# A hybrid encoder layer with 32 experts: gathering tokens from the fp32 residual rows, and a shorter way from the residual to the choice of experts

## The reference

```
n = rms_norm(x, mix_norm_g);  z = n @ w_in               # 1024 x 2336
o = concat(GLA(z), GQA(z))                               # two groups of heads, 1024 wide
h = x + o @ w_out                                        # 1024 x 1024
m = rms_norm(h, ffn_norm_g)
logits = m @ w_router + b_router                         # 32 experts
top_val, top_idx = top_k(logits, 4); gates = softmax(top_val)
for each token and each of its 4 experts e:
    u = m @ w1[e] + b1[e]                                # 1024 x 2048
    a = min(u[:1024], 7); b = clip(u[1024:], -7, 7)
    y += gate * ((a * sigmoid(1.702 a) * (b + 1)) @ w2[e] + b2[e])   # 1024 x 1024
out = rms_norm(h + y, final_norm_g)
```

## Time and profile before

| | |
|---|---|
| median of 3 runs | 1094.7 us (1090.6 to 1095.1) |
| profiled execution, its own time | 1092.27 us |
| its span, first to last instruction | 1090.3 us |
| mean granted TensorE clock | 0.986 |
| TensorE busy, matmuls | 983.2 us, 90% |
| VectorE, ScalarE, GpSimd busy | 230.1, 117.4, 20.3 us |
| moved by DMA | 421.31 MB, mean 386 GB/s |

### The profile page before, as it was taken

How to read it: one execution, slowest core, us unless ns; L and a number is a source line. 1 busy time by engine, 2 the same in 40 slices (tenths; PEclk the granted TensorE clock), 3 DMA queues, 4 the chain that set the end, 5 groups by cost and what they waited for, 6 DMA issues and landing times.

```text
span 1090.3 us, 13890 instructions
## 1 busy us (share of the span) xinstructions
PE 983.2 (90%) x5869; PEld 425.6 (39%) x5869; DVE 230.1 (21%) x531; ACT 117.4 (11%) x226; POOL 20.3 (2%) x24
## 2 busy tenths in 40 slices
PE   6997878999999999988889888998988888898885
PEld 4644544344444444433333333333333333333332
DVE  1577344111111111111111001111111111110113
ACT  1053130000000000000000000000000000000002
POOL 0010020000000000000000000000000000000000
PEclk9998998999999999999999999999999999999998
DMA  9924746999999999999999999999999999999993
GB/s 319 287 110 209 308 154 253 429 421 417 394 426 426 429 427 429 429 427 429 429 429 428 429 428 429 428 429 429 429 429 428 429 428 429 428 429 429 429 429 161
DMA packets 33093, 421.31 MB, mean 386 GB/s; under 512 B 4880, under 2 KB 5136, under 8 KB 7376
## 3 DMA queue, kind: packets, MB, share of 16 engines
q1 hardware_dynamic: 33072, 421.02, 92.6%
HBM read 419.95 MB, written 1.05 MB: 386 GB/s over the span
## 4 chain that ended last, share of the span: by engine, by line
PE 49%; DMA 42%; DVE 5%; ACT 2%; issue 1%; POOL 0%; SPq 0%; POOLq 0%; DVEq 0%
DMA ring<-in_w_dram 41%; PE bank L1354 20%; PE bank L1388 12%; PE bank L1057 4%; PE bank L1325 3%; PE bank L1318 3%; PE bank L1265 1%; PE bank L1370 1%; ACT work L573 1%; PE bank L1253 1%; PE bank L1274 1%; DMA h<-in_x_dram 1%; ACT work L522 1%; PE bank L1198 0%; PE bank L1143 0%
## 5 line engine op out<-in xcount | busy, mean ns | idle before, releaser
L1354 PE MATMUL bank<-ring,work 128*64 128x512 f32 x2016 | 458.0, 598 | 51.2 <-DMA ring<-in_w_dram 50.0
L1354 PEld LDWEIGHTS bank<-ring,work 128*64 128x64 f32 x2016 | 166.6, 136 | 324.2 <-issue 210.7
L1388 PE MATMUL bank<-ring,work 128*64 128x512 f32 x1024 | 226.8, 595 | 15.5 <-ACT work L573 15.5
L975 DVE TENSOR_SCALAR work<-bank 128x512 f32<-128x512 f32 x32 | 22.1, 692 | 726.9 <-PE bank L1354 726.9
L1388 PEld LDWEIGHTS bank<-ring,work 128*64 128x64 f32 x1024 | 71.2, 137 | 150.5 <-issue 132.9
L570 ACT ACTIVATE work<-work 128x512 f32<-128x512 f32 x32 | 20.2, 632 | 539.1 <-DVE work L975 539.1
L1325 PE MATMUL bank<-work 64*128 64x512 f32 x256 | 63.6, 615 | 0.7 <-ACT work L581 0.7
L1318 PE MATMUL bank<-work,tok 128*128 128x64 bf16 x1056 | 50.8, 194 | 0.0
L1318 PE MATMUL bank<-work 128*128 128x64 bf16 x528 | 49.0, 195 | 1.2 <-DVE work L948 1.2
L1318 PEld LDWEIGHTS bank<-work,tok 128*128 128x128 bf16 x1056 | 47.4, 99 | 0.0
L1318 PEld LDWEIGHTS bank<-work 128*128 128x128 bf16 x528 | 33.7, 99 | 27.2 <-issue 27.2
(11 more groups left out here) (190 smaller groups left out, 487.8 us busy)
## 6 DMA issues: line engine op xcount, KB each, us to landing
ring<-in_w_dram SPq DMA_DIRECT2D x190, 2048.0 KB, 33.1
ring<-in_w_in_dram SPq DMA_DIRECT2D x8, 1168.0 KB, 18.7
work<-in_w_dram SPq DMA_DIRECT2D x2, 2048.0 KB, 12.0
ring<-in_w_out_dram SPq DMA_DIRECT2D x2, 1024.0 KB, 14.5
ring<-in_w_out_dram SPq DMA_DIRECT2D x1, 2048.0 KB, 21.1
h<-in_x_dram SPq DMA_DIRECT2D x2, 512.0 KB, 4.7
out_dram<-tok SPq DMA_DIRECT2D x4, 256.0 KB, 2.4
tok<-in_b_dram SPq DMA_DIRECT2D x3, 256.0 KB, 16.6
```

The costliest lines, as they stand in the source:

```text
L975: nc.vector.tensor_scalar(glu, bank[2][:, :], LIMIT, None, ALU.min).then_inc(S.glu_ready, 1)
L1354: last = mm(bank[(2, 5)[g]][j * CAP:(j + 1) * CAP, :], xg[:, k * CAP:(k + 1) * CAP], chunk[:, r, g * FF + j * FG:g * FF + (j + 1) * FG], s ...
L1388: last = mm(bank[6][j * CAP:(j + 1) * CAP, :], hidT[:, r, s * CAP:(s + 1) * CAP], chunk[:, r, j * 512:(j + 1) * 512], start=s == 0 and r == 0,
```

## The change

The rows are no longer normalised and split. The gather takes the fp32 residual rows `h` themselves as weights, and the one-hot matrix, now fp32, holds 1/rms of its token instead of 1. So a gather is 8 pieces x 2 tiles = 16 fp32 matmuls. The first gather writes its two halves to two banks, and each half is taken out by itself, so that W1 may start with the first; the turn of the gates moves behind the first W1 chunk.

The output projection announces each of its four results; `h` is added, squared and turned by halves. Turned h goes to `tok`. The router is turned round: for each half tile four matmuls with 128x32 weights (the router's) and 128 columns (turned h), on four groups of 32 columns of the array; a fifth matmul with a 0/1 matrix `pick` adds the four groups and brings tokens back to partitions. The choice is made per tile: four sentinels of 3e38 stand behind the 32 logits, so the maximum eight are the four sentinels and the four highest logits, and match-and-replace marks these. `before_b` and `ones_b` come as bf16 from the host, the selection table is `pick`, and `ckeep` is loaded in two parts.

```diff
-            sp.dma_start(ckeep, c_keep).then_inc(S.ident_in, 16)
+            sp.dma_start(ident, c_keep[:, 0:P]).then_inc(S.ident_in, 16)
...
+                    sp.dma_start(ckeep[:, P:], c_keep[:, P:]).then_inc(S.const_in, 16)
...
-            sp.wait_ge(S.h_ps, TILES)
+            sp.wait_ge(S.h_ps, 2 * TILES)
             first_ring(7)
...
+            pool.memset(ones, 1.0).then_inc(S.marks, 1)
+            pool.memset(logit[:, :, EXPERTS:], SENTINEL).then_inc(S.marks, 1)
...
-                    pool.tensor_tensor(left[:, 0, :], tok[:, 0, :], parts[0][0], ALU.subtract).then_inc(S.left1, 1)
...
-                pool.tensor_tensor(parts[t][2], left[:, t, :], parts[t][1], ALU.subtract).then_inc(S.part2, 1)
...
+            square(0, 0)
+            square(0, 1)
+            turned_out(0, 1, 1)
+            square(1, 0)
+            turned_out(1, 0, 7)
+            router_parts(0)
+            square(1, 1)
+            router_parts(1)
...
+            def choose(t):
+
+                dve.wait_ge(S.logit_ps, t + 1)
+                dve.wait_ge(S.rstd2, t + 1)
+                step(nc.vector.scalar_tensor_tensor(logit[:, t, 0:EXPERTS], bank[PARTS_BANK[t]][:, SEQ:SEQ + EXPERTS],
+                                                    stat[:, 4 + t:5 + t], router_b, ALU.mult, ALU.add))
+                step(nc.vector.max(top[:, t, :], logit[:, t, :]))
+                nc.vector.tensor_scalar(stat[:, 6 + t:7 + t], top[:, t, TOP_K:TOP_K + 1], -1.0, None, ALU.mult).then_inc(S.top_done, 1)
+                step(nc.vector.match_replace(picked[:, t, :], top[:, t, :], logit[:, t, :], -SENTINEL))
+                nc.vector.tensor_scalar(chosen[:, t, :], picked[:, t, 0:EXPERTS], -SENTINEL, None, ALU.is_equal)\
+                    .then_inc(S.chosen_done, 1)
+
+            bias_select(0)
+            dve.wait_ge(S.pairs_in, 16 * GROUPS * W1_ROWS)
+            add_h(0, 0)
+            add_h(0, 1)
+            mean_square(0)
+            add_h(1, 0)
+            turned_out(0, 0, 0)
+            add_h(1, 1)
+            turned_out(1, 1, 4)
+            mean_square(1)
+            dve.wait_ge(S.marks, 2)
+            choose(0)
+            choose(1)
...
-            step(nc.vector.scalar_tensor_tensor(rank, ranks, 1.0, chosen, ALU.add, ALU.mult))
-            step(nc.vector.tensor_scalar(rank_t[:, :, 0:EXPERTS], rank, -1.0, None, ALU.add))
+            step(nc.vector.scalar_tensor_tensor(rank_t[:, :, 0:EXPERTS], ranks, 1.0, chosen, ALU.add, ALU.mult))
...
-                    last = nc.vector.tensor_scalar(onehot[:, t, :], iota[:, 0:CAP], rank_t[:, t, bass.ds(n, 1)], None,
-                                                   ALU.is_equal)
+                    last = nc.vector.tensor_scalar(onehot[:, t, :], slots[:, 0:CAP], rank_t[:, t, bass.ds(n, 1)],
+                                                   stat[:, 4 + t:5 + t], ALU.is_equal, ALU.mult)
...
+            def router_round(t, half):
+
+                pe.wait_ge(*((S.hT_v, 1), (S.hT_a, 1), (S.hT_a, 2), (S.hT_v, 2))[2 * t + half])
+                for j in range(4):
+                    k = half * 4 + j
+                    last = mm(bank[PARTS_BANK[t]][j * EXPERTS:(j + 1) * EXPERTS, 0:P], wr_sb[:, k, :], hT[:, k, t * P:(t + 1) * P],
+                              start=half == 0, stop=half == 1, skip_group_check=True)
+                if half == 1:
+                    last.then_inc(S.parts_ps, 1)
+
+            def router_sum(t):
+
+                pe.wait_ge(S.part_sb_done, t + 1)
+                mm(bank[PARTS_BANK[t]][:, SEQ:SEQ + EXPERTS], part_sb[:, t, :], pick[:, 0:EXPERTS], start=True, stop=True)\
+                    .then_inc(S.logit_ps, 1)
...
+            out_gla(0, 0, range(4))
+            out_gla(0, 1, range(4))
+            pe.wait_ge(S.glaT_a, 1)
+            out_gla(1, 0, range(4))
+            turn_h(0, 0)
+            turn_h(0, 1)
+            out_gla(1, 1, range(3))
+            turn_h(1, 0)
+            out_gla(1, 1, range(3, 4))
...
+            router_round(0, 0)
+            router_round(0, 1)
+            router_round(1, 0)
+            turn_h(1, 1)
+            router_sum(0)
+            router_round(1, 1)
+            router_sum(1)
+            start_hidden(0)
...
                 for k in range(KD):
                     c, r = divmod(k, W1_ROWS)
-                    for i in range(PARTS):
-                        for t in range(TILES):
-                            piece = parts[t][i].rearrange("p (c m r) -> p c m r", m=P, r=W1_ROWS)[:, c, :, r]
-                            last = mm(bank[6][:, k * CAP:(k + 1) * CAP], piece, onehot[:, t, :],
-                                      start=i == 0 and t == 0, stop=i == PARTS - 1 and t == TILES - 1)
+                    b = 3 if first and k < KD // 2 else 6
+                    for t in range(TILES):
+                        piece = h[:, t, :].rearrange("p (c m r) -> p c m r", m=P, r=W1_ROWS)[:, c, :, r]
+                        last = mm(bank[b][:, k * CAP:(k + 1) * CAP], piece, onehot[:, t, :],
+                                  start=t == 0, stop=t == TILES - 1)
+                    if first and k == KD // 2 - 1:
+                        last.then_inc(S.half_gathered, 1)
...
+                    if first and c == 0:
+                        turn_gates()
...
-            gather(0)
-            turn_gates()
+            gather(0, first=True)
```

More of the change, by code:

```diff
@@ L117, in encoder_layer @@
         tok = sb("tok", [P, TILES, D])
-        ckeep = sb("ckeep", [P, 4 * P])
-        ident, iota, before, ones = (ckeep[:, i * P:(i + 1) * P] for i in range(4))
+        ckeep = sb("ckeep", [P, 3 * P + TABLE])
+        ident, slots = ckeep[:, 0:P], ckeep[:, P:2 * P]
+        pick = ckeep[:, 2 * P:2 * P + TABLE]
+        before_b, ones_b = (ckeep[:, 2 * P + TABLE + i * (P // 2):2 * P + TABLE + (i + 1) * (P // 2)].bitcast(BF16)
+                            for i in range(2))
         biases = sb("biases", [P, D])
@@ L173, in encoder_layer @@
         q_g, k_g, head_g, router_b = row[:, 0:DH], row[:, DH:2 * DH], row[:, 2 * DH:2 * DH + DV], row[:, 2 * DH + DV:]
+        logit = front(TILES, EXPERTS + TOP_K)
+        top = front(TILES, 8)
+        picked = front(TILES, EXPERTS + TOP_K)
         assert front.at <= WORK
+        ones = qkT[:, 0, 0:P]
         reuse = Carve(work, at_raw)
@@ L562, in _, with square @@
-            act.wait_ge(S.top_done, 1)
-            for t in range(TILES):
-                nc.scalar.activation(weight[:, t, :], logit[:, t, :], ACT.Exp, bias=stat[:, 6 + t:7 + t])\
+            def square(t, nb):
+                act.wait_ge(S.h_done, 2 * t + nb + 1)
+                cols = slice(nb * 512, (nb + 1) * 512)
+                nc.scalar.activation(squares[:, t, cols], h[:, t, cols], ACT.Square,
+                                     accum_out=stat[:, 8 + 2 * t + nb:9 + 2 * t + nb]).then_inc(S.hsq, 1)
@@ L565, in _ @@
+            square(0, 0)
[6 more added lines that the diff above has]
+            router_parts(1)
+            for t in range(TILES):
+                act.wait_ge(S.top_done, t + 1)
+                nc.scalar.activation(weight[:, t, :], logit[:, t, 0:EXPERTS], ACT.Exp, bias=stat[:, 6 + t:7 + t])\
                     .then_inc(S.wexp_done, 1)
@@ L887, in _ @@
-            step(last)
-            for t in range(TILES):
-                last = nc.vector.max(top[:, t, :], logit[:, t, :])
-            step(last)
-            for t in range(TILES):
-                last = nc.vector.tensor_scalar(stat[:, 6 + t:7 + t], top[:, t, 0:1], -1.0, None, ALU.mult)
-            last.then_inc(S.top_done, 1)
-            topu = topi.bitcast(U32).rearrange("p (t k) -> p t k", k=8)
-            for t in range(TILES):
-                last = nc.vector.max_index(topu[:, t, :], top[:, t, :], logit[:, t, :])
@@ L904, in _, with bias_select, add_h @@
[L904 to L909 removed]
+            def bias_select(n):
+                nc.vector.tensor_scalar(sel, slots[0:B_ROWS, 0:CAP], 0.0, pick[0:B_ROWS, bass.ds(n, 1)], ALU.mult, ALU.add)\
+                    .then_inc(S.sel_ready, 1)
+            def add_h(t, nb):
+                dve.wait_ge(S.h_ps, 2 * t + nb + 1)
+                cols = slice(nb * 512, (nb + 1) * 512)
+                nc.vector.tensor_tensor(h[:, t, cols], bank[Y[2 * t + nb]][:, :], h[:, t, cols], ALU.add).then_inc(S.h_done, 1)
@@ L1306, in start_row, with gather @@
                    start=True, stop=False, skip_group_check=True)
-            def gather(n):
+            def gather(n, first=False):
                 pe.wait_ge(S.onehot_ready, n + 1)
```

241 lines of the change are left out of this document (89 added, 152 removed).

## The result

The changed kernel takes 1100.34 us (median of 6 runs, 1098.16 to 1102.67) against 1091.12 us of the kernel before (6 runs, 1090.23 to 1095.1); the ratio is 1.0069, 95% interval 1.0044 to 1.0095. So it is slower, by about 0.7%, and the interval lies clear of 1. The forecast was 1097 within 1090 to 1103; "within 0.5%" was held likelier (0.65) than "slower by more" (0.25), and the measured ratio lies on the side held less likely. The profiled execution took 1098.97 us, its span is 1097.2 us, 6.9 more than before's.

What follows compares the result with a forecast made beforehand. Weight transfers bound nearly all of the loop; TensorE decides only up to the fourth expert's mid-W2 and in the tail. There -0.45 - 4.7 + 6.85 = +1.7, tail +2.0, together +3.7 us: 1096.0, forecast 1097, range 1090 to 1103.

Steps and rivals of the forecast that it cites:

- the gate: Middle of the fourth expert's W2, 274.2 us before: what moves it moves the end; the change adds +1.7 us there.
- the hole before it: Underfed DMA queue before the fourth expert's W2 ends its first half: grows from some 3 us to 8 or 10.
- the front's gain given back: From start to first W1: what is won there, -0.45 and -4.7 us, five gathers give back.
- (b): Start: 192 KB fewer constants ahead of x, so x lands earlier: -0.45 us (0 to -0.6).
- (c): Output projection, turns and router: a router round on four column groups takes 0.47 us (0.2 to 0.94); sum matmul at 156.85.
- (d): Choice of experts: 1.0 us a tile, so the first gather starts at 159.4 us, not 165.34.
- (e): First gather to first W1: 5.25 us, half the gather at half clock; W1 at 164.65 instead of 169.32, -4.7.
- (a): Gather: 32 fp32 records at 0.109 us, 3.5 us (3.4 to 3.8) for 1.51; +0.85 and 3 x 2.0, tail +2.0.
- tail: Behind the last W1 chunk TensorE, not the transfers, decides; the longer gather there adds +2.0 us.
- 5 g - 8.7: Early experts and the end: what a gather of g us costs before the fourth expert's mid-W2 and after the last W1.
- R2: Rival, whole loop: TensorE becomes the bound, from a gather of 4.06 us; in all +52, 1147 us; chance 0.10.
- R3: Rival, front: it does not shorten (serial rounds, slow replacement, cold gather); +8 to +10, 1102 to 1105 us; chance 0.08.

Runs made afterwards that it cites:

- Experiment 5: Changed kernel with only the first gather on fp32 rows, the others on three bf16 parts made during the first W1: 1090.71 us, ratio 0.9982 to the kernel before.
- Experiment 4: Changed kernel with ten bf16 128x512 matmuls, results unread, in TensorE's gaps between router and first gather: 1096.7 us, ratio 1.0052 to the kernel before.
- experiments 0 and 7: 0: the changed kernel again, no edit, 1101.26 us; 7: the changed kernel with ckeep loaded whole ahead of the second half of x, 1100.15 us.

## Why the prediction was right, and where its sizes were off

The mechanism held where the end is decided: the gate, the hole before it (8.1 us; 8 to 10 expected), the gather's price on five places, the weights' rate behind it, the front's gain given back. The sum did not: +3.7 us expected, +6.9 in the profiled executions. That the time still fell inside the range owes something to luck, for errors of both signs partly cancel, and the gather (3.91 for 3.4 to 3.8) and the first W1 (6.2 us earlier for 4 to 6) lie just outside what I had named as signs of being right. By its steps, each the change of the time from one start to the next:

| step | expected | measured |
|---|---|---|
| (b) start, to the projection | -0.45 | 135.54 - 137.64 = -2.1 |
| (c), (d) projection to first gather | -5.95 | 20.97 - 27.70 = -6.7 |
| (e) first gather to first W1 | +1.27 | 6.61 - 3.98 = +2.6 |
| (a) first W1 to first W2 | +0.85 | 21.71 - 18.23 = +3.5 |
| (a) three experts more, to the gate | +6.0 | 90.32 - 83.10 = +7.2 |
| tail | +2.0 | +2.4 |

(a) The term that was mis-sized first is the gather. I put it at 0.109 us a record, near the router's row, and held 0.118 to be the upper bound; it is 0.122, 3.91 us, just outside my 3.8. In the five places of 5 g - 8.7 and in the first gather this is 6 x 0.41 = +2.5 us. It also brought R2 within reach: its threshold was 4.06 us, and the wait for weights fell to 2.3 us of the "15 or less". Experiment 5 took fp32 out of all gathers but one and won 10.55 us. That is in line with what the Trainium skill ("TensorE: Matmul & The Clock Gate", section "Weight-path perf modes — Fast Weight Load (FWL) and DoubleRow") says, that fp32 weights go without the fast weight load; no run here measures that load by itself.

(e) I took half of the gather at the half clock and nothing beyond it. The clock was at 0.50 from 157 to 167 us, for all but the first half microsecond of the gather (156.51 to 163.19) and for most of the first W1 chunk (to 168.85): 2.77 + 2.18 = 4.95 us instead of 1.75, +3.2 us. Experiment 4 shows it: with the gaps filled 4.8 us came back at the gate. It fell with no gap over 0.9 us (the longest, before the gather, is 0.86), after five microseconds in which TensorE was about half busy (2.67 us from 152 to 157), and it stayed down through ten microseconds of full work, where I had given it half of the gather.

(b) The step failed in its reason. I read that the constants' wait ends with the router weights, took it for cover, and priced the landing of x. It is the chain: 40.31 + 14.1 = 54.41 us before. In the changed kernel the router weights landed 2.3 us sooner and x 1.5 us sooner (6.38 for 7.88). For x it goes with the change: it landed at 6.4 to 7.2 us in the nine profiled executions that load ckeep in two parts and at 7.5 to 7.9 in the three that load it whole. For the router weights it isn't shown: 38.0 to 40.0 us in eight executions with two parts, 40.3 and 41.5 in two with one, and the medians of experiments 0 and 7 do not differ clearly.

(c), (d) The rounds on four column groups took 0.79 us for three, not 1.4: 24 records at 0.033, or 0.26 a round, where I had put 0.47 between bounds of 0.2 (all four side by side) and 0.94. It is also under the 0.4 that I had estimated from the Trainium skill's figure for three column tiles ("TensorE: Matmul & The Clock Gate", section "Part 3: Packing small matmuls — row/col tiling"). Match-and-replace was like the index search (0.18 us for 0.19), and the choice for a tile took 1.1 us for the 1.0 estimated. VectorE's list of the changed kernel, second tile:
```profile
154.32 0.25 DVE L868 SCALAR_TENSOR_TENSOR work<-bank,stat,work 128x32 f32<-128x32 f32 x1
154.61 0.20 DVE L870 MAX8 work<-work 128x8 f32<-128x36 f32 x1
...
154.98 0.18 DVE L872 MATCH_REPLACE8 work<-work 128x36 f32<-128x36 f32 x1
155.19 0.18 DVE L873 TENSOR_SCALAR work<-work 128x32 bf16<-128x32 f32 x1
```

So +2.5 and +3.2 against me, 1.65 (b) and 0.8 (c, d) for me: together +3.2, the difference between 3.7 and 6.9. R3 is out with that, since the front did shorten, by 8.8 us to the first gather. The forecast of "no change" as likelier than "slower" came from the first two. The medians differ by 9 us rather than 6.9; the ratio's 0.6 to 0.7% is 7 to 7.5 us, and the rest is the spread of the front, of which two sources were found (how long the half clock lasts, in the attention and at the first gather, and when the router weights land) and not apportioned.

## What to carry to other kernels

When a transfer bounds most of a kernel, look for the last point at which it still waits for the engine, and price only what lies before that point and behind the last transfer: here 4 gathers were worth 5.7 us and 28 were worth 2.5. The same operation may deserve two forms: the fp32 gather pays once, where it spares a wait for the split, and the bf16 one in the loop, where the split is hidden. And when a chain has been shortened until TensorE works only about half of the time, look at the granted clock behind it: here the half clock took back almost 5 us of what the front had won, and ten cheap matmuls in the gaps gave it back.

## What the runs showed of the hardware

- An fp32 record with 128x128 weights took 0.122 us with 64 columns (0.116 with weights that are neighbours in memory), 0.106 with 32. So an fp32 matmul of this shape costs 0.24 us where a bf16 one costs 0.031: three bf16 parts, three times the matmuls, are 2.6 times faster.
- Fp32 matmuls with 128x32 weights and 128 columns, four on the four column groups, took 0.033 us a record; with 128x128 weights and 128 columns a record takes 0.125 (GLA's output, 2.00 us for 16).
- The granted clock fell from 2.4 to 1.2 GHz with no idle gap longer than 0.86 us. Ten matmuls of 128x512 in bf16, put into the gaps, held it, and delayed nothing (20.98 us from the projection to the gather for 20.97).
